# A 31-tap depthwise convolution: from diagonal matrices per tap to four time phases on TensorE, relaid by DMA

## What is computed

```python
def conv_module(xn, w_in, b_in, dw_w, dw_b, ln_g, ln_b, w_out):
    h = xn @ w_in + b_in                       # 1024 -> 2048
    a, gate = jnp.split(h, 2, axis=-1)
    h = a * jax.nn.sigmoid(gate)               # 512 x 1024
    h = lax.conv_general_dilated(              # depthwise, causal, 31 taps
        h, dw_w[:, None, :], window_strides=(1,), padding=[(CONV_WIDTH - 1, 0)],
        dimension_numbers=('NWC', 'WIO', 'NWC'), feature_group_count=D_CONV) + dw_b
    h = jax.nn.silu(layernorm(h, ln_g, ln_b))
    return h @ w_out
```

## Time and profile before

| | us |
|---|---|
| median of 3 runs | 3435.8 |
| the profiled execution | 3438.27 |
| its span | 3436.5 |
| PE busy (share of the span) | 3361.7 (98%) |
| DVE busy | 2206.5 (64%) |
| ACT busy | 1480.1 (43%) |
| mean granted TensorE clock (1 = 2.4 GHz) | 0.995 |
| DMA | 315 MB, 92 GB/s on average |

### The profile page before, as it was taken

One profiled execution on the slowest core, in us unless ns is written; L12 is line 12 of the kernel. 1 busy time (PEld: TensorE's weight loads), 2 busy tenths in 40 slices (PEclk: granted clock), 3 DMA queues, 4 the chain that ended last, 5 costly groups with the idle time before them and its releaser, 6 DMA issues. The chain is left out here.

```text
span 3436.5 us, 42093 instructions
## 1 busy us (share of the span) xinstructions
PE 3361.7 (98%) x16655; PEld 2806.8 (82%) x16655; DVE 2206.5 (64%) x3574; ACT 1480.1 (43%) x2585; POOL 253.1 (7%) x319
## 2 busy tenths in 40 slices
PE   9999999999999999999999998999999999999999
PEld 8888888888788888888887777888888887888887
DVE  5644566788855545677788695544666696545665
ACT  4543333444335433334444554534333565543332
POOL 1300210000032002000001020100000000100000
PEclk9999999999999999999999999999999999999999
DMA  4111342323232123422322222413331312312332
GB/s 161 56 56 58 112 153 74 108 98 111 83 109 62 50 86 96 156 62 98 111 99 83 70 77 74 138 62 111 111 111 60 107 34 81 116 56 99 110 105 68
DMA packets 84149, 315.14 MB, mean 92 GB/s; under 512 B 10096, under 2 KB 10864, under 8 KB 78832
## 3 DMA queue, kind: packets, MB, share of 16 engines
q1 hardware_dynamic: 83952, 312.46, 27.9%
HBM read 308.23 MB, written 4.19 MB: 91 GB/s over the span
## 5 line engine op out<-in xcount | busy, mean ns | idle before, releaser
L1333 PE MATMUL bk<-xh,wh 128*128 128x512 f32 (+1 forms) x2216 | 836.9, 378 | 5.7 <-DVE xl L2065 5.6
L1333 PE MATMUL bk<-xh,wl 128*128 128x512 f32 (+1 forms) x2216 | 829.2, 374 | 0.0
L1333 PE MATMUL bk<-xl,wh 128*128 128x512 f32 (+1 forms) x2216 | 828.6, 374 | 0.0
L2052 DVE TENSOR_TENSOR wl<-wr,wh 128x1024 fp32r<-128x1024 f32 (+1 forms) x300 | 361.1, 1214 | 296.5 <-ACT wh L1641 295.5
L1333 PEld LDWEIGHTS bk<-xh,wh 128*128 128x128 f32 x2216 | 417.2, 188 | 79.3 <-issue 4.1
L1333 PEld LDWEIGHTS bk<-xh,wl 128*128 128x128 f32 x2216 | 416.9, 188 | 75.8
L1333 PEld LDWEIGHTS bk<-xl,wh 128*128 128x128 f32 x2216 | 417.3, 188 | 72.1
L1641 ACT ACTIVATE wh<-wr 128x1024 fp32r<-128x1024 f32 (+1 forms) x300 | 310.6, 1044 | 328.8 <-PE bk L1333 218.6
L2058 DVE SCALAR_TENSOR_TENSOR wl<-wr,par,wh 128x512 fp32r<-128x512 f32 (+1 forms) x360 | 249.4, 738 | 165.7 <-ACT wh L1647 164.4
L1647 ACT ACTIVATE wh<-wr,par 128x512 fp32r<-128x512 f32 (+1 forms) x360 | 236.1, 710 | 239.0 <-PE bk L1333 206.3
L1612 ACT ACTIVATE wh<-ar 128x1024 fp32r<-128x1024 f32 (+1 forms) x168 | 142.2, 846 | 397.7 <-DVE ar L2023 276.2
(11 more groups left out here) (295 smaller groups left out, 5366.6 us busy)
## 6 DMA issues: line engine op xcount, KB each, us to landing
wr<-in_wpk SPq DMA_DIRECT2D x468, 512.0 KB, 3.6
ar<-in_wdn SPq DMA_DIRECT2D x36, 1024.0 KB, 6.4
gb<-in_ln_g SPq DMA_DIRECT2D x6, 512.0 KB, 4.1
gb<-in_ln_b SPq DMA_DIRECT2D x6, 512.0 KB, 6.5
ar<-in_xT SPq DMA_DIRECT2D x8, 256.0 KB, 6.1
wr<-in_wpk SPq DMA_DIRECT2D x8, 256.0 KB, 4.9
ar<-in_memT SPq DMA_DIRECT2D x2, 1024.0 KB, 4.7
x<-in_x SPq DMA_DIRECT2D x4, 512.0 KB, 5.4
```

What stands on the lines that cost most here:

```text
L1333: i = pe.e.matmul(dst, lw, rw, start=g not in opened, stop=end)
L2052: dve.e.tensor_tensor(m.wl[:, s, a], m.wr[:, r, a], m.wh[:, s, a].bitcast(F32), ALU.subtract) \
```

## The change

TensorE takes five blocks (3 to 7), DVE three (0, 1 as a pair and 2). The five blocks are convolved in **four time phases**. `evac` writes such a block not as `hT` but as `hP`, with the positions ordered by phase (`in_time`: position 4t+q is put at q*128+t). SP stores it to DRAM (`phase_put`) and loads it back by four DMAs (`phase_get`) into `ph`, where the partitions are 4 phases x 32 channels and the free axis holds 4 channel groups of 136 columns (8 zeros ahead). One matmul then has a weight matrix of 128 x 128 that joins 4 input phases to 4 output phases for 32 channels, and 9 shifts of it make all 31 taps of one channel group (`conv_pe`): 9 plain fp32 matmuls of 128x128 with 128 columns per group, 4 groups per block, 20 groups in all. The weight matrices are made on the host (`tz`, 20 of 128 x 1152 fp32, 576 KB each) and loaded by SP (`tz_load`), group 0 into a buffer of its own and the others in turn into three. ACT evacuates each bank in four pieces (`conv_pe_ev`), and SP stores it to DRAM and loads it back channel-major by four DMAs (`phase_out`). `y` is kept in phase order for all eight blocks; DVE and ACT put it back in time order when they write `ah` and `al`. The diagonals, the split of the weights and the split of the blocks are gone. `mem2_split` and `mem2_low` move forward, to about two steps behind block 0; the memory is loaded into `gb` instead of `ar`.

```diff
-PEC = (5, 6, 7)
-TAPS = 31 * len(PEC)
+PEC = (3, 4, 5, 6, 7)
+SHIFTS = 9
...
         def convs():
-            for pair in ((0, 1), (2, 3), (4,)):
+            for pair in ((0, 1), (2,)):
...
         def on_pe():
...
+            while 0 not in ready:
+                yield
+            self.add("mem2_load", si + 1)
+            self.add("tz_load", 0)
+            yield
+            yield
+            self.add("mem2_split", si + 1)
+            self.add("mem2_low", si + 1)
+            yield
+            self.add("tz_load", 1)
             for q, m in enumerate(PEC):
                 while m not in ready:
                     yield
-                self.add("conv_pe_split", m, q)
...
+                self.add("phase_put", m, q)
+                yield
+                if q < 2:
+                    self.add("phase_get", m, q)
+            self.add("tz_load", 2)
+            self.add("tz_load", 3)
             for q, m in enumerate(PEC):
...
+                bank = self.take()
+                for g in range(4):
+                    self.add("conv_pe", m, q, g, bank)
+                    if 0 < 4 * q + g < 4 * len(PEC) - 3:
+                        self.add("tz_load", 4 * q + g + 3)
+                    if g % 2:
                         yield
...
+                self.add("conv_pe_ev", m, q, bank)
+                self.give(bank)
+                if q + 2 < len(PEC):
+                    self.add("phase_get", PEC[q + 2], q + 2)
+                self.add("phase_out", m, q)
+            self.conv_g = self.take()
+            for n, ch in enumerate((0, 1, 3, 4, 5)):
+                self.add("conv_mean", self.conv_g, ch, n == 0, False)
         self.add("conv_start")
         drive((proj(), 1), (convs(), 1), (on_pe(), 1))
         later = []
+        self.add("c2_loads", 1)
...
-        self.add("conv_mean", self.conv_g, 7, False, False)
+        self.add("conv_mean", self.conv_g, 2, False, False)
+        self.add("conv_mean", self.conv_g, 6, False, False)
         fill(2)
-        self.add("conv_mean", self.conv_g, 4, False, True)
+        self.add("conv_mean", self.conv_g, 7, False, True)
...
+def tz_at(n):
+    return 1 + (n - 1) % 3 if n else 0
...
+    def conv_pe(ch, q, g, bank):
+        if g == 0:
+            begin(bank)
+            pe.wait_ge(*ev["phase_in", ch])
+        n = 4 * q + g
+        pe.wait_ge(*ev["d_tz", n])
+        for h in range(SHIFTS):
+            i = pe.e.matmul(bk[sc.bank[bank]][:, tile(g)], m.tz[tz_at(n)][:, tile(h)], m.ph[q % 2][:, g, h:h + 128],
+                            start=h == 0, stop=h == SHIFTS - 1)
+        i.then_inc(*ev.up("pe_at", ("tz_used", n), *([("grp", bank), ("phase_used", q)] if g == 3 else [])))
...
+    def conv_pe_ev(ch, q, bank):
+        ps = psum(bank)
+        if q >= 2:
+            act.wait_ge(*ev["d_ys", q - 2])
+        for g in range(4):
+            i = act.e.activation(m.yst[q % 2][:, tile(g)], ps[:, tile(g)], ACT.Identity, bias=m.p("dw_bp", 4 * q + g, 1),
+                                 scale=1.0)
+        i.then_inc(*ev.up("act_ev", ("free", bank), ("conv_ps", ch)))
...
-        act.e.activation(m.ah[:, ch, :], m.y[:, ch, :], ACT.Silu, bias=bias, scale=scale)
+        act.e.activation(m.ah[:, ch, :].rearrange("p (t q) -> p q t", q=4),
+                         m.y[:, ch, :].rearrange("p (q t) -> p q t", q=4), ACT.Silu, bias=bias, scale=scale)
...
-        dve.e.tensor_tensor(m.al[:, ch, :], m.y[:, ch, :], m.ah[:, ch, :].bitcast(F32), ALU.subtract) \
+        dve.e.tensor_tensor(m.by_four(m.al[:, ch, :]), m.in_time(m.y[:, ch, :]), m.by_four(m.ah[:, ch, :].bitcast(F32)),
+                            ALU.subtract) \
...
+    def tz_load(n):
+        sp.wait_ge(*ev[("xs", CONVMOD, 3, 4) if n == 0 else ("mem", CONVMOD + 1) if n == 1 else ("hT", 7) if n < 4 else
+                       ("tz_used", n - 3)])
+        b = tz_at(n)
+        sp.e.dma_start(m.tz[b], ins["tz"][n, :, :]).then_inc(*ev.up(f"d_tz{b}", ("d_tz", n), by=16))
+
+    def phase_put(ch, q):
+        sp.wait_ge(*ev["hT", ch])
+        sp.e.dma_start(m.hs[q, :, :], m.hP[q]).then_inc(*ev.up("d_hs", ("d_hs", q), by=16))
+
+    def phase_get(ch, q):
+        sp.wait_ge(*ev["d_hs", q])
+        sp.wait_ge(*ev["conv_zero"])
+        if q >= 2:
+            sp.wait_ge(*ev["phase_used", q - 2])
+        src = m.hs[q, :, :].rearrange("(g c) (p t) -> p c g t", g=4, p=4)
+        for p in range(4):
+            sp.e.dma_start(m.ph[q % 2][32 * p:32 * p + 32, :, 8:136], src[p]) \
+                .then_inc(*ev.up(f"d_ph{q % 2}", *([("phase_in", ch)] if p == 3 else []), by=16))
+
+    def phase_out(ch, q):
+        sp.wait_ge(*ev["conv_ps", ch])
+        sp.e.dma_start(m.ys[q, :, :], m.yst[q % 2]).then_inc(*ev.up("d_ys", ("d_ys", q), by=16))
+        sp.wait_ge(*ev["d_ys", q])
+        if ch in (6, 7):
+            sp.wait_ge(*ev["conv_y", ch - 6])
+        src = m.ys[q, :, :].rearrange("(p c) (g t) -> g c p t", g=4, p=4)
+        for g in range(4):
+            sp.e.dma_start(m.y[32 * g:32 * g + 32, ch, :].rearrange("c (p t) -> c p t", p=4), src[g]) \
+                .then_inc(*ev.up("d_yb", *([("conv_y", ch)] if g == 3 else []), by=16))
```

More of the change, by code:

```diff
@@ L916, in convs @@
                     yield
-                if pair == (4,):
-                    self.add("mem2_low", si + 1)
                 self.add("conv0", pair)
@@ L926, in convs @@
                         yield
-            self.add("conv_join", 4)
+            self.add("conv_join", 2)
         def on_pe():
[L930 to L938, removed]
+            while 0 not in ready:
[8 more added lines that the diff above has]
+            self.add("tz_load", 1)
             for q, m in enumerate(PEC):
@@ L1074, in __init__ @@
         self.parked = nc.dram_tensor("park", (S, D), F32, kind="Internal").ap()
+        self.hs = nc.dram_tensor("phase_in", (len(PEC), 128, S), F32, kind="Internal").ap()
+        self.ys = nc.dram_tensor("phase_out", (len(PEC), 128, S), F32, kind="Internal").ap()
         sb = lambda n, s, d=F32: ctx.enter_context(nc.sbuf_tensor(n, s, d))
@@ L1145, in __init__ @@
         self.po = self.gbf[:, 1536:2048]
-        self.hT = u(0, 8 * 542).rearrange("p (k s) -> p k s", k=8)
+        self.hT = u(0, 3 * 542).rearrange("p (k s) -> p k s", k=3)
+        self.hP = [u(1626 + 512 * q, 512) for q in range(len(PEC))]
+        self.ph = [u(12016 + 544 * q, 544).rearrange("p (g t) -> p g t", g=4) for q in range(2)]
+        self.halo = u(12016, 1088).rearrange("p (g t) -> p g t", g=8)[:, :, 0:8]
+        self.yst = [u(13104 + 512 * q, 512) for q in range(2)]
         self.y = u(4336, 4096).rearrange("p (k s) -> p k s", k=8)
@@ L1151, in __init__ @@
         self.ysum = u(11504, 512)
-        flat = lambda a: a[:, 0:8, :].rearrange("p k s -> p (k s)")
-        self.oh, self.ol = ([flat(a)[:, q * 542:q * 542 + 542] for q in range(len(PEC))] for a in (self.ah, self.al))
-        self.dwh, self.dwl = self.ah[:, 4, 0:248], self.al[:, 4, 0:248]
+        w = 128 * SHIFTS
+        self.tz = [u(5872, w), self.gbf[:, 0:w], u(8432, w), u(9584, w)]
         self.cmu, self.crs, self.cvar = u(8432, 512), u(8944, 512), u(10992, 512)
@@ L1219, in crow, with in_time, by_four @@
         return self.crms(2 + h // 2, t)[:, h % 2:h % 2 + 1]
[L1221 to L1225, removed]
+    def in_time(self, a):
+        return a.rearrange("p (q t) -> p t q", q=4)
+    def by_four(self, a):
+        return a.rearrange("p (t q) -> p t q", q=4)
     def mrow(self, which, t):
@@ L2760, in sync_program @@
                 mem_load=mem_load, back=back, m2_loads=m2_loads, pool_loads=pool_loads, mem2_load=mem2_load,
-                c2_loads=c2_loads, store=store, down_load=down_load, finish=finish)
+                c2_loads=c2_loads, tz_load=tz_load, phase_put=phase_put, phase_get=phase_get, phase_out=phase_out, store=store, down_load=down_load, finish=finish)
     for kind, *args in sc.items:
@@ L2883, in lay_out @@
         put(n, cols(g[k]))
+    put("dw_bp", np.tile(g["conv_dw_b_2"].reshape(8, 4, 32)[3:].reshape(20, 1, 32), (1, 4, 1)).reshape(20, 128).T)
     a["par"] = par
+    w = g["conv_dw_w_2"][0].reshape(31, 8, 4, 32)[:, 3:].reshape(31, 20, 32)
+    tz = np.zeros((20, 4, 32, SHIFTS, 4, 32), np.float32)
+    for h in range(SHIFTS):
+        for q in range(4):
+            for p in range(4):
+                k = 4 * h + q - p - 2
+                if 0 <= k < 31:
+                    tz[:, q, np.arange(32), h, p, np.arange(32)] = w[k]
+    a["tz"] = tz.reshape(20, 128, 128 * SHIFTS)
     a["cst"] = tables()
```

86 lines of the change are left out of this document (23 added, 63 removed).

## The result

The kernel after takes **3443.66 us** in the median (3441.2 to 3445.81, 11 runs), the one before 3435.8 (3434.8 to 3438.06, 11 runs) beside it: a ratio of 1.0022, 95% interval 1.0014 to 1.003. The change costs 7.9 us. The forecast was 3435.9 with a range of 3425 to 3450. The profiled execution took 3444.43 us, its span is 3442.6; against 3436.5 the span is 6.1 us longer.

What follows compares the result with a forecast made beforehand. PE (98% busy) and DVE bound the kernel side by side. PE's 24.4 us saving goes to four idle times (17.2), the clock (6.4) and the start (1.3); with strides +0.4, net +0.1: median 3435.9 us, range 3425 to 3450.

Steps and rivals of the forecast that it cites:

- likeliest case: Taps on PE: idle times eat the gain; chance 0.48, own range 3429 to 3442 us.
- PE's saving: Taps on PE: 65.0 us replaced by 40.6 us for 20 groups, saving 24.4 us if PE alone counted.
- The mechanism: SP's order at block ends: the wait for the store precedes load 4b+7, so PE idles 4.3 us, four times.
- The turn: From one block's end to the next: 12.4 us, 14.0 with the clock's fall; the fourth 11.75 before the clock.
- the store from issue to landing: SP's store of phase_out in each turn: 2.3 us taken, bounds 2.0 and 3.2.
- The clock: Last group of each block: falls to half clock after each idle time, +1.6 us a turn, 6.4 in all.
- The start: First block on PE: load 2 waits for the last evacuation and lands late, a wait of 1.3 us.
- The tail: After the last block: block 7's relay takes 9.1 us against 8.6 of PE work; the last mean waits 0.5.
- The strides: Behind the taps: DVE's low part, strided by 512 B, costs +0.4 us, between 0.69 and 1.22.
- The issues don't stretch: Rival on SP: relay loads take 0.80 us per issue, 10.4 us more, giving 3446 to 3452; chance 0.22.
- The hidden relay: Rival in the taps' stretch: PE stays full, taps end 22.8 us earlier, 3413 us; chance 0.05.
- That alone would just pass: Weight loads on DMA: 576 KB per 2.03 us group needs 290 GB/s, against 360 in the best window.

Runs made afterwards that it cites:

- the last two runs: Kernel before with one of three matmuls per tap on PE: 3438.78 us; kernel before with 26 of block 4's DVE taps left out: 3434.5 us.
- the floor run: Changed kernel with five weight buffers, loads back two weight loads later, and 256 KB instead of 576 per weight load (part of the weights left out): 3411.86 us.
- The order alone: Changed kernel with SP issuing the four loads back of a block's output two weight loads later, nothing else changed: 3425.68 us, ratio 0.9969.
- The 256 KB runs: Weight loads of 256 KB instead of 576: in the changed kernel 3430.32 us; with five buffers and loads back two weight loads later 3411.86 us.
- The fillers: Changed kernel with 22, 22, 22 and 13 extra overwritten matmuls before groups 7, 11, 15 and 19 to keep PE busy: 3439.26 us, ratio 1.0008.
- the run of both: Changed kernel with five rotating weight buffers instead of three and the loads back two weight loads later: 3417.85 us, ratio 0.9948.
- the one on ACT's queue: Changed kernel with five buffers and later loads back, ACT instead of SP issuing the relay's gets, stores and loads back: 3424.63 us, ratio 0.9962.
- the run without strides: Changed kernel with conv_out writing ah and al in phase order, without the reordering: 3442.04 us, ratio 1.0018.

## Why the prediction was right, and which terms were off

The measured 3443.7 us lies in the range of 3425 to 3450 and 7.8 us above the forecast. It does not lie in the range that the prediction gave to its own likeliest case, 3429 to 3442. That upper end was summed too low: with the landings at their upper bounds (1.7 us a turn) and the clock at its own (0.4 a turn) the prediction's terms give 3444.4.

**What bounds the kernel: right.** PE and DVE were two bounds side by side; the last two runs show it for each. PE's saving was right too: 40.6 us predicted for 20 groups, 40.2 in the floor run, and DVE was done at 2803.9, predicted 2803 to 2805.

**The mechanism: right.** The order alone wins back 18.0 us. The stops lie before groups 7, 11, 15 and 19, each ended by a load of `tz`. They are 19.0 us together. The prediction's 17.2 took 4.3 four times, though its own fourth turn of 11.75 leaves 3.6 there, and 16.4 in all. From the start of a store to the next weight load it took 5.0 to 6.4 us, not 4 to 5, which is the next point.

**The turn: mis-sized by two landings.** From the end of one block to the end of the next (2782.7, 2800.1, 2815.7, 2832.1, 2844.5) the turns are 17.4, 15.6, 16.4 and 12.4 us, together 61.8; predicted were 14.0 three times and 13.35, together 55.4. Term by term over the four turns (a block's end is the start of PE's next group, or, for the third, the release of SP's next load):

| term | predicted | measured |
|---|---|---|
| end of block to the store's issue | 8.0 | 8.7 |
| store to landing, with semaphores | 4 x (2.3 + 0.3) = 10.4 | 4.65 + 3.25 + 3.42 + 3.36 = 14.7 |
| four loads back issued | 6.9 | 7.6 |
| weight load to PE's start | 4 x 3.9 = 15.6 | 4.5 + 4.0 + 4.3 + 3.7 = 16.5 |
| group and clock | 4 x (2.03 + 1.6) = 14.5 | 4.0 + 4.1 + 4.0 + 2.1 = 14.2 |

The mis-sized term is "the store from issue to landing", with 2.3 us taken and bounds of 2.0 and 3.2. The four landed after 4.6, 3.2, 3.4 and 3.3 us: one far above the upper bound, the others at it or up to 0.2 above. With the semaphores it makes 4.3 of the 6.4 us. The rows of before had only a store with nothing beside it; here it stands behind a weight load and, in three of the turns, four gets. The 256 KB runs show it from the other side: less in flight, 2.4 us.

**The clock: the right sign, too large.** In three turns the clock fell, after idle times of 5.07 us and more, and in the fourth, after 3.09 us, it did not. The Trainium skill ("TensorE: Matmul & The Clock Gate", HAM oscillation) has such a loop throttled in every turn; this trace agrees in three of four. The fillers put a price on it: 4.4 us, not 6.4. As the prediction gave it a fall in each turn at 1.6 us, this error hid a part of the store's.

**The start: right in size.** The wait before group 2 was 1.35 us, predicted 1.3. The stop of 1.47 us before group 6 was not foreseen. It cost nothing in the first turn, which SP's chain sets, not PE's.

**The tail: the right number by luck.** From the end of the last block to the start of the last mean it took 8.8 us, predicted 9.1. But the prediction let the mean wait for block 7's relay, and PE doesn't wait there. The four last loads back landed in 2.0 us, not 4.0 (bounds 3.5 and 4.4), so that the relay took about 6.7 us, and what counts is PE's own work, predicted at 8.6.

**The strides: 0.4 predicted, 1.1 by the waits in the traces.** DVE's strided line took 1.10 us, near the upper bound of 1.22, and ACT's write, which the prediction priced at no more than that, added 0.5. To lean on DVE's unstrided row as the nearest was the wrong choice.

**The rivals.** The issues don't stretch: an issue on SP took 0.33 to 0.48 us, in one row of four 0.56. The hidden relay would have given 3413; the floor run reaches 3412, but only with fewer bytes. One step on the way was wrong without harm to the forecast: the 290 GB/s of which it said "That alone would just pass" count the weights alone, and the 360 that they were held against is one window of 1 us. The relay of a block moves 256 KB four times, 1.05 MB in 8.1 us or 129 GB/s, which makes 419 together. The fullest slices of about 2 us carry 421 to 423, but the windows of 10 us with a DMA share of 0.99 to 1.04, in the run of both and the one on ACT's queue, carry 327 to 373. By this estimate the design asks for more than the DMA sustained here while PE runs full, and with 4/9 of the weight bytes the 3.9 us of idle time of the best version are gone.

**The sum.** The last mean ends 7.0 us later than predicted (2854.3, not 2847.3). Behind it lie 588.3 us and not the 588.9 of before with 0.4 added, so the profiled execution took 6.0 more than predicted, 3444.4 and not 3438.4. The other 1.7 us come from the step to the median: the prediction took off the 2.5 us by which the profiled execution of before stood above its median, and the one of after stands only 0.8 above. The forecast for the median was off by 7.8 us, 0.23%; the interval of the ratio (0.14 to 0.3%) lies on both sides of the 0.2% that the prediction called the limit, so that the change is slower for certain, but not for certain by that much. The next version to build is the one with five buffers and the later loads back, 3417.85 us.

## What to carry to other kernels

Where a queue is worked in program order, look for a wait inside an item and count everything behind it. Here one wait for a store per block cost 18 us in all, and moving it behind two loads that don't depend on it turned a loss into a gain. Take the landing of a store from a row in which the same loads are in flight, and where there is none, let the upper bound reach well beyond the row of a lone one. When work moves from an engine to DMA, add up all the bytes of a turn, the relays' too, before comparing them with what a trace carries over a whole turn, not in its best microsecond. And before counting a saving, ask which second engine ends at the same time: cutting PE or DVE alone was worth nothing here, cutting both up to 24 us (in the floor run, which leaves out weights).

## What was not expected of the hardware

- **A store's landing grows with what is in flight.** The same 256 KB took 2.0 us alone, 2.4 and 2.5 beside loads of 256 KB, 3.25 to 3.42 behind one of 576 KB, 4.65 behind two, 4.7 in the median in the run of both, and 6.0 to 6.2 with five buffers and the old order or from a second queue. The first figure is the only one that the kernel before shows.
- **Strided accesses.** ACT writing with a step of 16 bytes took 1.32 us and not 0.81, DVE with a step of 512 bytes 1.10 and not 0.69, DVE's evacuation from PSUM 1.15 and not 0.75: 1.5 to 1.6 times each. The Trainium skill ("SBUF — State Buffer", Door 1) says that every access which goes to a new line pays a penalty; it gives no size, and these runs do, for these three patterns.
- **The clock after a stop.** The length of a stop alone doesn't decide. At 5.07 us and more the clock was granted in part at 1.2 GHz in the next 4 us. After the 2.19 us in the run of both, the next group took 3.6 us and not 2.0, and after 3.17 us with 256 KB loads two groups took 5.7. But after 3.09 us in the changed kernel, and 1.99 in the run of the order alone, it stayed at 2.4 GHz. Even the same wait at the same place went both ways: after 2.48 us in the kernel before it fell, after 2.49 us in the run without strides it stayed at 1.00. What the chip looks at besides was not tried.
